# Sums of squares on VectorE for three means, and a pipelined embedding gate, in a two-layer decoder step

## Chip, cores and metric

The kernel runs on one core of one Trainium2 chip. The metric is the time on the device in microseconds (us), as the median of three executions. Beside those there is one profiled execution, from which all rows below come. TensorE is called PE, VectorE DVE, ScalarE ACT, GpSimd POOL and SyncE SP in the rows; PEld is TensorE's loading of weights.

## What is computed

The reference runs two layers of a decoder over 264 tokens (256 of a prompt, 8 single tokens) with a model width of 1024. In each layer a normalised input goes through one projection into three mixers, a shared output projection and a residual add; then comes a feed-forward block (dense in layer 0, eight experts in layer 1), and last an embedding gate. What the change touches is where the means of the squares for the norms are formed:

```python
def rmsnorm(x, g):
    xf = x.astype(jnp.float32)
    y = xf * lax.rsqrt(jnp.mean(xf * xf, axis=-1, keepdims=True) + EPS)
    return (y * g.astype(jnp.float32)).astype(x.dtype)
...
    h = h + y @ w_o
    h = h + ffn(rmsnorm(h, g_ffn))
    h = h + jax.nn.sigmoid(rmsnorm(h, g_ple) @ w_ple_gate) * (p_i @ w_ple_proj)
```

## The kernel before

The features lie on the 128 partitions, so that the state `h` is eight tiles ("chunks") of 128x264. The weights stream through a ring of three 2 MB slots in SBUF, in the order of their use. The mixers' projections of both layers and the output projection of layer 0 multiply the streamed weights as they are (`project_fp32`, L710). The others split each quarter of a slot first: ScalarE writes a rounded copy `whi` (L961), VectorE the remainder `wlo` (L1361, called by `low_upto`), three quarters ahead of TensorE, and `project` takes three products for each block (L734, L737, L738). The order of the work on each engine is the order in which the code of that engine is written; engines meet through semaphores.

A mean of squares goes over all 1024 features, that is over the partitions and over the eight chunks. ScalarE writes the square of each chunk into `sq`; `average` (L745) then multiplies the eight tiles of `sq` with a constant matrix of 1/1024 and sums them in one bank of PSUM. Each fp32 product shows as two passes in the trace, so a mean is 16 rows of L750. ScalarE takes the root (L944), VectorE its reciprocal (L1376), and the next block's results are scaled by it only when they are evacuated from PSUM (L1383, four banks in turn). So TensorE goes on with the next block's products right after `average` and needs for them only the gained rows of `h`, not the mean itself.

Three places matter, all at the end of a block of layer 0 or of the gate:

- **Boundary 1**, output projection to feed-forward block. For each chunk VectorE adds the result to `h` (`add_to_h`, L1388), writes the gained rows in two parts (`gain`, L1367 and L1368), and ScalarE squares the chunk (L1069).
- **Boundary 2**, feed-forward block to embedding gate: the same with ScalarE's L1094.
- **Boundary 3**, embedding gate of layer 0 to the mixers of layer 1. For each chunk VectorE evacuates the gate's product (`gate_out`, L1383), ScalarE takes the sigmoid (L1133), VectorE multiplies (L1701), adds to `h` (L1703) and writes the gained row for layer 1 (`mix_gain`, L1372); ScalarE squares (L1136, the last chunk L1142). In layer 0 VectorE evacuates chunk k and waits for its sigmoid before it does anything else. In layer 1 it evacuates chunk k+1 ahead of the rest of chunk k, and ScalarE loads the table of the root (L1140) before the last square instead of after it.

```python
for k in range(KD):                          # VectorE, embedding gate
    if l == 0 or k == 0:
        gate_out(k)
    if l and k + 1 < KD:
        low_upto(min(k + AHEAD + 1, KD), tail)
        gate_out(k + 1)
    dve.wait_ge(S["sig_ple"], k + 1)
    link(nc.vector.tensor_tensor(pp[:, k, :], pp[:, k, :], sig[:, k % 2, :], ALU.mult))
```

`link` makes VectorE wait for its own instruction before it issues the next.

Of the kernel before, what the change touches and what calls it, by code (L numbers as in the profile page):

```python
# [29 lines left out]
ALU = mybir.AluOpType  # L30
ACT = mybir.ActivationFunctionType
# [3 lines left out]
D_MODEL, SEQ, DEPTH, NB = 1024, 256, 2, 8  # L35
# [6 lines left out]
T = SEQ + NB  # L42
KD = D_MODEL // P
# [21 lines left out]
AHEAD = SPLITS - 1  # L65
# [80 lines left out]
def dense_quarters(chunk):  # L146

    return splits(min(NEED[chunk] + AHEAD, DENSE_Q))
# [7 lines left out]
def build(nc, wstream, x_in, p_in, par_in, state_in, y_out, a_prompt, a_sample, c_prompt, c_sample, v_sample):  # L156
    xn_rows = nc.dram_tensor("xn_rows", [T, ROW], F32, kind="Internal").ap()
    y_rows = nc.dram_tensor("y_rows", [1 + UNITS * CAP, D_MODEL], F32, kind="Internal").ap()
    with ExitStack() as ctx:
# [3 lines left out]
        def sem(name):  # L163
            return ctx.enter_context(nc.semaphore(name))
# [14 lines left out]
        sq = sb("sq", [P, KD, T])  # L179
# [17 lines left out]
        ones = {d: sb(f"ones_{d}", [P, P]) for d in (D_MODEL, D_A, D_B, 1)}  # L197
        before = sb("before", [P, P])
        ident = sb("ident", [P, P])
        eps = sb("eps", [P, 1])  # L200
# [53 lines left out]
        warm = cut(2)  # L254
# [8 lines left out]
        bank = [ctx.enter_context(nc.psum_tensor(f"bank{i}", [P, 512], F32)) for i in range(8)]  # L263
# [19 lines left out]
        tail = {n: sem(f"{n}_tail") for n in ("hi", "lo", "used")}  # L283
# [2 lines left out]
        dve_step = sem("dve_step")  # L286
        stored = sem("stored")
        flag_ready = sem("flag_ready")
        y_gained, y_pool, y_out_stored = (sem(n) for n in ("y_gained", "y_products_by_gpsimd", "y_out_stored"))


# [395 lines left out]
        def _(pe):  # L687
# [57 lines left out]
            def average(out, d, srcs, signal, waits=None):  # L745

                for k, s in enumerate(srcs):
                    if waits:
                        pe.wait_ge(waits[0], waits[1] + k)
                    mm = pe.matmul(out[:, 0:T], ones[d][:, :], s, start=(k == 0), stop=(k == len(srcs) - 1))  # L750
                mm.then_inc(signal, 1)

            def both(a, b, n):
                return [a[:, k, :] for k in range(n)], [b[:, k, :] for k in range(n)]

# [5 lines left out]
            pe.wait_ge(consts, 13)  # L761
            for l in range(DEPTH):
                S, B = L[l], BASE[l]
                average(bank[4], D_MODEL, [sq[:, k, :] for k in range(KD)], S["ms"], (S["sq_mix"], 1))
                project_fp32(B["zc"], N_ZC, gz, S["gh_mix"])
                project_fp32(B["zab"], 2 * CB, gz)

# [42 lines left out]
                else:  # L810
# [3 lines left out]
                        route_chunk(pe, k - 1)  # L814
                    route_chunk(pe, KD - 1)
                    route(pe)
                average(bank[4], D_MODEL, [sq[:, k, :] for k in range(KD)], S["ms"], (S["sq_ffn"], 1))
                if l == 0:

                    hids = both(hid_hi, hid_lo, KH)  # L820
# [25 lines left out]
                    at[0] = 0  # L846

                if l == 0:
                    average(bank[4], D_MODEL, [sq[:, k, :] for k in range(KD)], S["ms"], (S["sq_ple"], 1))
                    project(B["ple"], KD, *ghs, S["gh_ple"])  # L850
                else:
                    def square_mean(k):

                        pe.wait_ge(S["sq_ple"], k + 1)
                        mm = pe.matmul(bank[4][:, 0:T], ones[D_MODEL][:, :], sq[:, k, :], start=(k == 0), stop=(k == KD - 1))
                        if k == KD - 1:
                            mm.then_inc(S["ms"], 1)

                    assert LAST_BANKS[0] == B["ple"] % BANKS and LAST_BANKS[1] == 4
                    project(B["ple"], 1, *ghs, S["gh_ple"], tail, after=lambda k: k and square_mean(k - 1))  # L860
                    square_mean(KD - 1)
                    project(B["ple"] + 1, KD - 1, *ghs, S=tail)
# [78 lines left out]
        def _(act):  # L941
# [50 lines left out]
            for l in range(DEPTH):  # L992
# [134 lines left out]
                for k in range(KD):  # L1127
# [6 lines left out]
                    if k:  # L1134
                        act.wait_ge(made, k)
                        nc.scalar.activation(sq[:, k - 1, :], h[:, k - 1, :], ACT.Square).then_inc(done, 1)  # L1136
                        if l:
                            final_rows(k - 1)
                if l:
                    nc.scalar.activation(warm[:, 0:1], eps[:, :], ACT.Sqrt)  # L1140
                act.wait_ge(made, KD)
                nc.scalar.activation(sq[:, KD - 1, :], h[:, KD - 1, :], ACT.Square).then_inc(done, 1)  # L1142
            final_rows(KD - 1)
# [194 lines left out]
        def _(dve):  # L1338
# [16 lines left out]
            def low_upto(n, S=dense):  # L1355

                for i in range(done_lo[0], n):
                    q = SPLIT_Q[i] if S is dense else (PRE_MOE + N_EXP * UNIT_SLOTS) * QUARTERS + i
                    at = (i + SPLIT_AT if S is dense else i) % SPLITS
                    dve.wait_ge(S["hi"], i + 1)  # L1360
                    nc.vector.tensor_tensor(wlo[:, at, :], quarter_at(q), whi[:, at, :].bitcast(F32),  # L1361
                                            ALU.subtract).then_inc(S["lo"], 1)
                done_lo[0] = max(done_lo[0], n)

            def gain(l, name, k, signal, hi=gh_hi, lo=gh_lo):

                link(nc.vector.tensor_scalar(hi[:, k, :], h[:, k, :], col(l, name, k), None, ALU.mult))  # L1367
                nc.vector.scalar_tensor_tensor(lo[:, k, :], h[:, k, :], col(l, name, k), hi[:, k, :].bitcast(F32),  # L1368
                                               ALU.mult, ALU.subtract).then_inc(signal, 1)

            def mix_gain(l, k):
                nc.vector.tensor_scalar(gz[k], h[:, k, :], col(l, "g_mix", k), None, ALU.mult).then_inc(L[l]["gh_mix"], 1)  # L1372

# [23 lines left out]
            for l in range(DEPTH):  # L1397
# [189 lines left out]
                for k in range(KD):  # L1587
                    q = k - (KD - AHEAD)
                    if l and q >= 0:
                        dve.wait_ge(M["hi"], q + 1)  # L1590
                        nc.vector.tensor_tensor(wlo[:, q, :], quarter_at(q), whi[:, q, :].bitcast(F32),
                                                ALU.subtract).then_inc(M["lo"], 1)
                    add_to_h(B["wo"] + k, k)
                    if l == 0:
                        gain(l, "g_ffn", k, S["gh_ffn"])
                    else:
                        if k == KD - CB:
                            dve.wait_ge(S["tails"], 1)
                        nc.vector.tensor_scalar(g_rows[k], h[:, k, :], col(l, "g_ffn", k), None,
                                                ALU.mult).then_inc(F["normed"], 1)  # L1600
                    low_upto(dense_quarters(B["wo"] + k))
# [3 lines left out]
                if l == 0:  # L1605
# [6 lines left out]
                    for half, (ff, down) in enumerate((("ff", "down"), ("ff2", "down2"))):  # L1612
                        for f in range(KH):
                            n = half * KH + f


                            if n >= 2:
                                dve.wait_ge(S["silu"], n - 1)
                            evacuate(B[ff] + 2 * f, up[:, n % 2, :])
                            if f:  # L1620
                                hidden_low(n - 1)
                            low_upto(dense_quarters(B[ff] + 2 * f))
                            evacuate(B[ff] + 2 * f + 1, zb[:, n % 2, :])
                            dve.wait_ge(acc_evac, B[ff] + 2 * f + 2)
                            dve.wait_ge(S["silu"], n + 1)
                            nc.vector.tensor_tensor(zb[:, 2 + n % 2, :], zb[:, n % 2, :], sig[:, n % 2, :],
                                                    ALU.mult).then_inc(S["hid_f32"], 1)
                            if f < KH - 1:
                                low_upto(dense_quarters(B[ff] + 2 * f + 1))
                        hidden_low(half * KH + KH - 1)  # L1630
                        low_upto(dense_quarters(B[ff] + KF - 1))
                        for k in range(KD):
                            add_to_h(B[down] + k, k)
                            if half:
                                gain(l, "g_ple", k, S["gh_ple"])
                            low_upto(dense_quarters(B[down] + k))
                else:
                    route_tokens(dve, link, S)
# [50 lines left out]
                def gate_out(k):  # L1689
                    if k >= 2:  # L1690
                        dve.wait_ge(S["sig_ple"], k - 1)
                    evacuate(B["ple"] + k, up[:, k % 2, :])

                for k in range(KD):
                    if l == 0 or k == 0:
                        gate_out(k)
                    if l and k + 1 < KD:
                        low_upto(min(k + AHEAD + 1, KD), tail)
                        gate_out(k + 1)
                    dve.wait_ge(S["sig_ple"], k + 1)  # L1700
                    link(nc.vector.tensor_tensor(pp[:, k, :], pp[:, k, :], sig[:, k % 2, :], ALU.mult))  # L1701
                    if l + 1 < DEPTH:
                        link(nc.vector.tensor_tensor(h[:, k, :], h[:, k, :], pp[:, k, :], ALU.add))  # L1703
                        mix_gain(l + 1, k)
                        low_upto(dense_quarters(B["ple"] + k))
                    else:
                        nc.vector.tensor_tensor(h[:, k, :], h[:, k, :], pp[:, k, :], ALU.add).then_inc(S["y_fin_h"], 1)
# [110 lines left out]
```

## Time and profile before

| | before |
|---|---|
| median of 3 executions | 1105.1 us (1104.42 to 1105.19) |
| profiled execution, time on the device | 1104.26 us |
| its span, first to last instruction | 1102.6 us |
| TensorE busy | 1075.9 us, 98% of the span |
| VectorE, ScalarE busy | 891.0 us, 669.4 us |
| mean granted clock of TensorE | 0.993 of full |

The profiled execution lies 0.84 us under the median, and 1.66 us of its time lie outside the span. A row of a timeline gives the start in us from the span's start, the duration, the engine, the line of the kernel, the operation and its tiles, and in brackets how long the engine stood idle before it and what ended that. A row that ends in x16 merges 16 like instructions. The granted clock is given as a share of full speed: 1.00 is 2.4 GHz, 0.50 is 1.2 GHz.

### The profile page before, as it was taken

To read this page: it belongs to the slowest core of one execution; us is meant where nothing else is said; L and a number is where in the kernel's file an instruction comes from. 1 tells how busy PE (TensorE), PEld (TensorE's weight loads), DVE (VectorE), ACT (ScalarE), POOL (GpSimd) and SP (SyncE) were. 2 spreads that over 40 slices of the span, in tenths; PEclk is the share of its full clock that TensorE was granted. 3 is DMA by queue.
4 is the path that set the end of the run, shared out by engine and by line. 5 is a ranking of instruction groups with operands and counts; after the bars stand their busy time and mean duration, and the time that the engine had idled before them with its cause. 6 is when DMAs were issued, how large, how long until landed. Compare 5 with 4: busy or idle time off the path is not lost.

```text
span 1102.6 us, 16235 instructions
## 1 busy us (share of the span) xinstructions
PE 1075.9 (98%) x5901; PEld 930.0 (84%) x5901; DVE 891.0 (81%) x1257; ACT 669.4 (61%) x840; POOL 43.7 (4%) x58
## 2 busy tenths in 40 slices
PE   9998999999999998899999999999999999999996
PEld 8887899999999887788888888888888888888785
DVE  5897566566667889659989999899998999999785
ACT  2204344344454123548888788888888888887674
POOL 1000000000000000000000010000100001001100
PEclk9999999999999999899999999999999999999998
DMA  8432644645542442438999999999999999999910
GB/s 335 152 145 79 229 153 164 261 153 178 196 163 86 160 153 78 153 116 336 370 358 392 369 392 377 350 407 366 381 373 353 415 361 380 376 360 420 366 78 40
DMA packets 24197, 291.50 MB, mean 264 GB/s; under 512 B 3160, under 2 KB 3192, under 8 KB 7376
## 3 DMA queue, kind: packets, MB, share of 16 engines
q1 hardware_dynamic: 21040, 280.32, 66.5%
q0 software_dynamic: 3104, 10.46, 2.7%
q8 instruction: 34, 0.56, 0.2%
q14 instruction: 19, 0.16, 0.0%
HBM read 283.98 MB, written 6.79 MB: 264 GB/s over the span
## 4 chain that ended last, share of the span: by engine, by line
PE 88%; DMA 4%; DVE 3%; issue 2%; ACT 1%; POOL 1%; SPq 0%; POOLq 0%; DVEq 0%; ACTq 0%
PE bank L664 15%; PE bank L710 14%; PE bank L668 14%; PE bank L667 14%; PE bank L734 8%; PE bank L737 8%; PE bank L738 8%; PE bank L750 2%; DMA sq<-y_rows,row_id 2%; DMA y_rows<-work 1%; PE bank L608 1%; DVE rstd L1376 1%; DMA ring<-wstream 1%; PE bank L592 1%; PE bank L573 1%
## 5 line engine op out<-in xcount | busy, mean ns | idle before, releaser
L1271 DVE TENSOR_TENSOR wlo<-ring,whi 128x1024 fp32r<-128x1024 f32 x384 | 460.0, 1220 | 50.9 <-ACT whi L880 44.1
L880 ACT ACTIVATE whi<-ring 128x1024 fp32r<-128x1024 f32 x384 | 404.6, 1059 | 87.2 <-PE bank L664 71.4
L664 PE MATMUL bank<-whi,gh_hi 128*128 128x512 f32 x512 | 204.4, 399 | 0.1
L668 PE MATMUL bank<-whi,gh_lo 128*128 128x512 f32 x512 | 199.8, 390 | 0.0
L667 PE MATMUL bank<-wlo,gh_hi 128*128 128x512 f32 x512 | 199.5, 390 | 0.0
L734 PE MATMUL bank<-gh_hi,whi 128*128 128x264 f32 x480 | 138.0, 288 | 0.0
L737 PE MATMUL bank<-gh_lo,whi 128*128 128x264 f32 x480 | 136.0, 283 | 0.0
L738 PE MATMUL bank<-gh_hi,wlo 128*128 128x264 f32 x480 | 135.9, 283 | 0.0
L664 PEld LDWEIGHTS bank<-whi,gh_hi 128*128 128x128 f32 x512 | 96.2, 188 | 21.8 <-DVE wlo L1271 3.4
L668 PEld LDWEIGHTS bank<-whi,gh_lo 128*128 128x128 f32 x512 | 96.1, 188 | 20.9
L961 ACT ACTIVATE whi<-ring 128x1024 fp32r<-128x1024 f32 x87 | 91.1, 1050 | 35.0 <-PE bank L734 28.7
L667 PEld LDWEIGHTS bank<-wlo,gh_hi 128*128 128x128 f32 x512 | 96.3, 188 | 18.4
L710 PE MATMUL bank<-gz,ring 128*128 128x264 f32 x456 | 107.9, 386 | 0.1
L1361 DVE TENSOR_TENSOR wlo<-ring,whi 128x1024 fp32r<-128x1024 f32 x87 | 105.3, 1218 | 0.3
L664 PE MATMUL bank<-whi,hid_hi 128*128 128x512 f32 x256 | 102.9, 402 | 1.3 <-DVE wlo L1271 1.3
L668 PE MATMUL bank<-whi,hid_lo 128*128 128x512 f32 x256 | 101.0, 395 | 0.0
L667 PE MATMUL bank<-wlo,hid_hi 128*128 128x512 f32 x256 | 100.8, 394 | 0.0
L710 PEld LDWEIGHTS bank<-gz,ring 128*128 128x128 f32 x456 | 86.5, 190 | 15.5 <-DMA ring<-wstream 0.8
L734 PEld LDWEIGHTS bank<-gh_hi,whi 128*128 128x128 f32 x480 | 90.4, 188 | 0.6 <-issue 0.3
L737 PEld LDWEIGHTS bank<-gh_lo,whi 128*128 128x128 f32 x480 | 90.5, 188 | 0.3
L738 PEld LDWEIGHTS bank<-gh_hi,wlo 128*128 128x128 f32 x480 | 90.0, 187 | 0.0
L1432 DVE SCALAR_TENSOR_TENSOR cv<-cpad,par,cv 128x256 f32<-128x256 f32 x180 | 76.9, 479 | 1.4
(253 smaller groups left out, 1371.6 us busy)
## 6 DMA issues: line engine op xcount, KB each, us to landing
ring<-wstream SPq DMA_DIRECT2D x130, 2048.0 KB, 8.5
y_rows<-work POOLq DMA_DIRECT2D x7, 512.0 KB, 8.0
ring<-wstream SPq DMA_DIRECT2D x1, 1536.0 KB, 10.4
h<-x_in SPq DMA_DIRECT2D x2, 528.0 KB, 4.1
y_out<-work SPq DMA_DIRECT2D x2, 528.0 KB, 3.0
xn_rows<-work SPq DMA_DIRECT2D x2, 512.5 KB
par<-par_in SPq DMA_DIRECT2D x2, 494.5 KB, 7.6
c_sample<-xc POOLq DMA_DIRECT2D x2, 372.0 KB, 3.9
```

The lines of the kernel that those rows point to most:

```text
L664: mm = pe.matmul(out[:, :], xh, whi[:, pos, cols_], start=(k == 0), stop=False)
L667: pe.matmul(out[:, :], xh, wlo[:, pos, cols_], start=False, stop=False)
L668: mm = pe.matmul(out[:, :], xl, whi[:, pos, cols_], start=False, stop=(k == last))
L710: mm = pe.matmul(bank[c % BANKS][:, 0:T], quarter_at(q)[:, w * P:(w + 1) * P], rows[k], start=(k == 0), stop=(k == len(rows) - 1))
L734: mm = pe.matmul(out, wh, hi[k], start=(k == 0), stop=False)
L737: pe.matmul(out, wh, lo[k], start=False, stop=False)
L738: mm = pe.matmul(out, wl, hi[k], start=False, stop=(k == len(hi) - 1))
L880: nc.scalar.activation(whi[:, q % SPLITS, :], quarter_at(q), ACT.Copy).then_inc(S["hi"], 1)
L961: nc.scalar.activation(whi[:, at, :], quarter_at(q), ACT.Copy).then_inc(S["hi"], 1)
L1271: v.tensor_tensor(wlo[:, q % SPLITS, :], quarter_at(q), whi[:, q % SPLITS, :].bitcast(F32), ALU.subtract).then_inc(S["lo"], 1)
L1361: nc.vector.tensor_tensor(wlo[:, at, :], quarter_at(q), whi[:, at, :].bitcast(F32), ALU.subtract).then_inc(S["lo"], 1)
L1432: last[c] = tick(nc.vector.scalar_tensor_tensor(dst, src, wc[:, c, k:k + 1], dst, ALU.mult, ALU.add))
```

## The change

VectorE gets a new step, `sum_square`, that adds a chunk's square into the first tile of `sq`, in place. At boundaries 1 and 2 it adds chunks 1 to 6, one per chunk, right behind `gain` of the following chunk; at boundary 3 it adds chunks 1 to 5, two chunks late. TensorE's new `average_of_sum` waits for the last of these sums and multiplies the sum and the chunks that are left, so two tiles at boundaries 1 and 2, three at boundary 3, in place of eight. The gate of layer 0 takes the order of layer 1: `gate_out(k + 1)` is issued ahead of the rest of chunk k. ScalarE loads the table of the root before the last square in layer 0 also. The means at the start of layer 0, in the feed-forward block of layer 1 and at the end stay as they were.

```diff
@@ TensorE
+            def average_of_sum(signal, ready, n=KD - 1):
+
+                sums[0] += n - 1
+                pe.wait_ge(sq_sum, sums[0])
+                pe.matmul(bank[4][:, 0:T], ones[D_MODEL][:, :], sq[:, 0, :], start=True, stop=False)
+                for k in range(n, KD):
+                    pe.wait_ge(ready, k + 1)
+                    mm = pe.matmul(bank[4][:, 0:T], ones[D_MODEL][:, :], sq[:, k, :], start=False, stop=(k == KD - 1))
+                mm.then_inc(signal, 1)
...
-                average(bank[4], D_MODEL, [sq[:, k, :] for k in range(KD)], S["ms"], (S["sq_mix"], 1))
+                if l == 0:
+                    average(bank[4], D_MODEL, [sq[:, k, :] for k in range(KD)], S["ms"], (S["sq_mix"], 1))
+                else:
+                    average_of_sum(S["ms"], S["sq_mix"], KD - 2)
...
-                average(bank[4], D_MODEL, [sq[:, k, :] for k in range(KD)], S["ms"], (S["sq_ffn"], 1))
+                if l == 0:
+                    average_of_sum(S["ms"], S["sq_ffn"])
+                else:
+                    average(bank[4], D_MODEL, [sq[:, k, :] for k in range(KD)], S["ms"], (S["sq_ffn"], 1))
...
-                    average(bank[4], D_MODEL, [sq[:, k, :] for k in range(KD)], S["ms"], (S["sq_ple"], 1))
+                    average_of_sum(S["ms"], S["sq_ple"])
@@ ScalarE
-                if l:
-                    nc.scalar.activation(warm[:, 0:1], eps[:, :], ACT.Sqrt)
+                nc.scalar.activation(warm[:, 0:1], eps[:, :], ACT.Sqrt)
                 act.wait_ge(made, KD)
                 nc.scalar.activation(sq[:, KD - 1, :], h[:, KD - 1, :], ACT.Square).then_inc(done, 1)
@@ VectorE
+            def sum_square(ready, k):
+
+                if 1 <= k < KD - 1:
+                    dve.wait_ge(ready, k + 1)
+                    if k > 1:
+                        dve.wait_ge(sq_sum, sums[0])
+                    sums[0] += 1
+                    nc.vector.tensor_tensor(sq[:, 0, :], sq[:, 0, :], sq[:, k, :], ALU.add).then_inc(sq_sum, 1)
...
                         gain(l, "g_ffn", k, S["gh_ffn"])
+                        sum_square(S["sq_ffn"], k - 1)
...
                                 gain(l, "g_ple", k, S["gh_ple"])
+                                sum_square(S["sq_ple"], k - 1)
...
                 for k in range(KD):
-                    if l == 0 or k == 0:
+                    if k == 0:
                         gate_out(k)
-                    if l and k + 1 < KD:
-                        low_upto(min(k + AHEAD + 1, KD), tail)
+                    if k + 1 < KD:
+                        if l:
+                            low_upto(min(k + AHEAD + 1, KD), tail)
                         gate_out(k + 1)
+                    if l == 0:
+                        low_upto(dense_quarters(B["ple"] + k))
+                        sum_square(L[1]["sq_mix"], k - 2)
                     dve.wait_ge(S["sig_ple"], k + 1)
```

On TensorE at boundary 1, before (the output projection, the mean, the first products of the feed-forward block):

```order
L710 MATMUL bank<-work,ring 128x264 x64
L750 MATMUL bank<-sq,ones 128x264 x8
L734 MATMUL bank<-gh_hi,whi 128x264
L737 MATMUL bank<-gh_lo,whi 128x264
L738 MATMUL bank<-gh_hi,wlo 128x264
```

and of the change:

```order
L711 MATMUL bank<-work,ring 128x264 x64
L760 MATMUL bank<-sq,ones 128x264
L763 MATMUL bank<-sq,ones 128x264
L735 MATMUL bank<-gh_hi,whi 128x264
L738 MATMUL bank<-gh_lo,whi 128x264
L739 MATMUL bank<-gh_hi,wlo 128x264
```

Six of the eight products of the mean are gone; the first that is left reads the sum.

On VectorE at boundary 3, the last two chunks of the gate of layer 0 (`up` is the evacuated product, `small` holds the gained rows of the last two chunks), before:

```order
L1383 TENSOR_TENSOR up<-bank,rstd 128x264
L1701 TENSOR_TENSOR pp<-pp,sig 128x264
L1703 TENSOR_TENSOR h<-h,pp 128x264
L1372 TENSOR_SCALAR small<-h,par 128x264
L1383 TENSOR_TENSOR up<-bank,rstd 128x264
L1701 TENSOR_TENSOR pp<-pp,sig 128x264
L1703 TENSOR_TENSOR h<-h,pp 128x264
L1372 TENSOR_SCALAR small<-h,par 128x264
```

and of the change:

```order
L1412 TENSOR_TENSOR up<-bank,rstd 128x264
L1398 TENSOR_TENSOR sq<-sq 128x264
L1736 TENSOR_TENSOR pp<-pp,sig 128x264
L1738 TENSOR_TENSOR h<-h,pp 128x264
L1401 TENSOR_SCALAR small<-h,par 128x264
L1398 TENSOR_TENSOR sq<-sq 128x264
L1736 TENSOR_TENSOR pp<-pp,sig 128x264
L1738 TENSOR_TENSOR h<-h,pp 128x264
L1401 TENSOR_SCALAR small<-h,par 128x264
```

The evacuation at the top of the second piece is that of the last chunk: the work of the last but one chunk now stands behind it, and two sums stand between.

## Rows read from the trace of the kernel before

**Rows 1.** Chain that ended last, in order of time (start, us, what): boundaries 1, 2.

```profile
127.30 3.56 PE bank L750 x16
322.68 3.56 PE bank L750 x16
```

**Rows 2.** Timeline of all engines, boundary 1.

```profile
127.13 3.72 PE L750 MATMUL bank<-sq,ones 128*128 128x264 f32 x16
...
128.19 0.49 DVE L1368 SCALAR_TENSOR_TENSOR gh_lo<-h,par,gh_hi 128x264 fp32r<-128x264 f32 x1
128.60 1.22 DVE L1361 TENSOR_TENSOR wlo<-ring,whi 128x1024 fp32r<-128x1024 f32 x1
130.50 0.48 PE L734 MATMUL bank<-gh_hi,whi 128*128 128x264 f32 x1
```

**Rows 3.** Timeline of DVE, boundary 2 and the gate of layer 0.

```profile
323.58 0.49 DVE L1368 SCALAR_TENSOR_TENSOR gh_lo<-h,par,gh_hi 128x264 fp32r<-128x264 f32 x1
...
343.68 0.43 DVE L1703 TENSOR_TENSOR h<-h,pp 128x264 f32<-128x264 f32 x1
344.15 0.36 DVE L1372 TENSOR_SCALAR gz<-h,par 128x264 f32<-128x264 f32 x1
344.42 1.22 DVE L1361 TENSOR_TENSOR wlo<-ring,whi 128x1024 fp32r<-128x1024 f32 x1
...
351.66 0.36 DVE L1372 TENSOR_SCALAR small<-h,par 128x264 f32<-128x264 f32 x1
```

**Rows 4.** Timeline of PE, from boundary 2 to the mixers of layer 1.

```profile
325.88 0.48 PE L734 MATMUL bank<-gh_hi,whi 128*128 128x264 f32 x1
...
349.16 0.28 PE L738 MATMUL bank<-gh_hi,wlo 128*128 128x264 f32 x1
349.28 3.96 PE L750 MATMUL bank<-sq,ones 128*128 128x264 f32 x16
353.08 2.83 PE L710 MATMUL bank<-gz,ring 128*128 128x264 f32 x12
```

**Rows 5.** Timeline of ACT, boundary 3.

```profile
352.05 0.42 ACT L1142 ACTIVATE sq<-h 128x264 f32<-128x264 f32 x1 [1.04 <-DVE small L1372]
352.49 1.28 ACT L944 ACT_TABLE_LOAD   x1
```

**Rows 6.** Timelines of PE, DVE and ACT, end of the gate of layer 1.

```profile
1088.20 0.28 PE L738 MATMUL bank<-gh_hi,wlo 128*128 128x264 f32 x1
...
1088.59 0.43 DVE L1383 TENSOR_TENSOR up<-bank,rstd 128x264 f32<-128x264 f32 x1 [1.66 <-PE bank L738]
1088.94 0.42 DVE L1701 TENSOR_TENSOR pp<-pp,sig 128x264 f32<-128x264 f32 x1
1089.39 0.43 DVE L1707 TENSOR_TENSOR h<-h,pp 128x264 f32<-128x264 f32 x1
...
1090.71 1.28 ACT L1140 ACT_TABLE_LOAD   x1
1092.00 0.20 ACT L1140 ACTIVATE small<-eps 128x1 f32<-128x1 f32 x1
1092.11 0.41 ACT L1142 ACTIVATE sq<-h 128x264 f32<-128x264 f32 x1
```

**Rows 7.** Timeline of PE, mixers of layer 1.

```profile
429.20 1.16 PE L710 MATMUL bank<-pe_in,ring 128*128 128x264 f32 x4 [2.10 <-DVE work L1383]
...
441.68 1.60 PE L750 MATMUL bank<-sq,ones 128*128 128x264 f32 x6 [0.82 <-ACT sq L1036]
445.98 0.59 PE L734 MATMUL bank<-hid_hi,whi 128*128 128x264 f32 x1 [2.70 <-ACT pp L972]
```

**Rows 8.** Windows: stretch, us, busy of five engines, PEclk, DMA share, GB/s.

```profile
430.00:435.00 5.00, 3.68 (x25) 3.10 (x24) 3.97 (x11) 2.87 (x6) 1.29 (x2) 1.00 0.05 8
...
445.00:446.00 1.00, 0.02 (x1) 0.03 (x1) 0.95 (x1) 0.92 (x4) 0.00 (x0) 0.78 0.99 426
...
452.00:453.00 1.00, 1.00 (x9) 1.00 (x8) 0.60 (x2) 0.17 (x1) 0.00 (x0) 0.80 0.02 4
```

More of the change, by code:

```diff
@@ L288, in build @@
         flag_ready = sem("flag_ready")
+        sq_sum = sem("squares_summed")
         y_gained, y_pool, y_out_stored = (sem(n) for n in ("y_gained", "y_products_by_gpsimd", "y_out_stored"))
@@ L751, in average @@
                 mm.then_inc(signal, 1)
+            sums = [0]
+            def average_of_sum(signal, ready, n=KD - 1):
[6 more added lines that the diff above has]
+                mm.then_inc(signal, 1)
             def both(a, b, n):
@@ L1369, in gain @@
                                                ALU.mult, ALU.subtract).then_inc(signal, 1)
+            sums = [0]
+            def sum_square(ready, k):
[5 more added lines that the diff above has]
+                    nc.vector.tensor_tensor(sq[:, 0, :], sq[:, 0, :], sq[:, k, :], ALU.add).then_inc(sq_sum, 1)
             def mix_gain(l, k):
```

## The prediction

> **What bounds the kernel now.** I read the chain that ended last first: both means at the ends of layer 0's blocks stand on it, with 3.56 us of TensorE each [rows 1]. So a pass of L750 costs 3.56 / 16 = 0.2225 us, a product of two passes 0.445 us. Then I read the timelines around the three boundaries, because a product taken off the chain only helps if TensorE has something else to do at that moment. At boundary 1 TensorE starts the mean at 127.13, while VectorE is still working on the last chunk: its `gh_lo` starts at 128.19, and the next block's first product runs at 130.50 [rows 2]. So the first products of the mean are done in time in which the last chunk is not ready anyway. At boundary 3 this is plainer: the gate's last product starts at 349.16 and ends at 349.44, the last gained row of VectorE starts at 351.66, its square ends at 352.05 + 0.42 = 352.47, and the mixers' first product starts at 353.08 [rows 3 to 5]. The mean and the mixers there wait for the last square, not for the number of products. From the release by that square to the next block's first product it takes 353.08 - 352.47 = 0.61 us with one product of the mean in between. The roots and reciprocals behind a mean are not on the path, since TensorE goes on into four free banks.
>
> **The change part by part.**
>
> *Boundaries 1 and 2.* TensorE now can't start before the sum of chunks 0 to 6, and that is VectorE's last instruction there. `gh_lo` takes 128.60 - 128.19 = 0.41 us until the next instruction starts [rows 2], so the sum starts at 128.60. The trace has no such sum; the nearest row is the add of two SBUF tiles of the same size into `h`, 0.43 us [rows 3], and I take that; its start-to-start step, 0.35 us as with the evacuation to the product in layer 1 [rows 6], is the lower bound where something follows. The sum ends at 129.03. With two products behind it, 0.61 + 0.445 = 1.06 us, the next block starts at 130.09 instead of 130.50: **-0.41 us**. At boundary 2 the sum starts at 323.58 + 0.41 = 323.99, ends at 324.42, and the gate starts at 325.48 instead of 325.88 [rows 3, 4]: **-0.40 us**. The five earlier sums of each boundary lie in time in which VectorE waits for TensorE; without that cover each would cost its 0.35 to 0.43 us. The remainder `wlo` that follows the sum starts 0.43 us later, and is made three quarters ahead: nothing.
>
> *Boundary 3, the order of the gate.* The end of layer 1's gate shows this order without sums. I count from the end of the gate's last product. The last evacuation starts at 1088.59 - (1088.20 + 0.28) = 0.11 [rows 6]. Behind it on VectorE stand, in order: a sum (at 0.11 + 0.35 = 0.46), the product of chunk 6 (0.81), the add (0.81 + 0.45 = 1.26, the step 1089.39 - 1088.94 of [rows 6]), the gained row (1.26 + 0.47 = 1.73, the step 344.15 - 343.68 of [rows 3]), the last sum (0.27 later, 344.42 - 344.15, so 2.00 to 2.43), the product of chunk 7 (2.35), the add (2.80), the gained row (3.27 to 3.63). Before, chunk 6 was already finished when chunk 7 was evacuated. ScalarE can square chunk 6 when its gained row ends, at 1.73 + 0.36 = 2.09: 2.13 to 2.55. Then comes the table, 1.28 us [rows 5, 6], from 2.57 to 3.85, the one-element root 0.01 behind it, and the last square 0.11 after that (1092.11 - 1092.00): 3.97 to 4.39. The mixers start 0.61 later, at 5.00, where before they start at 353.08 - 349.44 = 3.64: **+1.36 us**. Of this 0.31 is the table, which now stands ahead of the last square; without it the square would end at 3.63 + 0.03 + 0.42 = 4.08. The rest is the two sums and the product, add and gained row of chunk 6 that now stand behind the last evacuation. The 1.28 us saved behind the mean buy nothing, since the root is off the path.
>
> Within the gate, VectorE's work for a chunk is 0.35 + 1.22 + 0.35 + 0.45 + 0.47 + 0.27 = 3.11 us against TensorE's 24 products of 0.12 (349.28 - 349.16 [rows 4]) = 2.9 us. It falls behind by 0.2 per chunk over the two chunks that have both a sum and a split. The split for chunk k+3 now starts when chunk k+1 is done and takes 0.35 + 1.22 = 1.6 of the 2.9 us that chunk k+2 runs: covered; if that were wrong, TensorE would stall by up to 0.5.
>
> Here a rule of the skill speaks against the early table. The instruction behind the load of layer 1 starts 0.01 us after its end [rows 6]. The Trainium skill (ScalarE: Activation LUTs, "What ACT_TABLE_LOAD costs") adds a drain of about 1.38 us to every load; by that the last square would come 1.38 us later still and the sum would be 1.9 instead of 0.55. The row decides.
>
> So the plain sum is -0.41 - 0.40 + 1.36 = **+0.55 us**.
>
> *What the idle time does to TensorE's clock.* This is the larger term. At boundary 3 TensorE now has nothing to multiply from 0 to the last sum's end at 2.43, plus about 0.2 for loading weights: 2.6 to 2.7 us, then a short burst, then it waits again. The trace has three waits to hold beside that. After 2.10 us of idle at 429.20, and after 0.82 at 441.68, the granted clock stayed at 1.00; around 2.70 us of idle, from 443.28 (441.68 + 1.60) to 445.98, it fell to 0.50 [rows 7, 8]. The windows date it: 0.78 in the stretch from 445 gives a fall at 445.56, 0.80 in the one from 452 a rise at 452.40. That is 6.84 us at half speed, beginning 2.28 us into the wait. Boundary 3's wait is nearest to the one of 2.70, so I take the clock to fall there in the same way: half speed from 2.28 to 9.12. On the path in it lies what follows the last square, from about 4.6 to 9.12; 4.5 us at half speed lose 2.25. Bounds: 0 if the clock holds, 6.84 / 2 = 3.4 if all of it falls into unbroken work. At boundaries 1 and 2 TensorE idles from 127.30 [rows 1] to about 129.25, 1.95 us, nearest to the 2.10 that left the clock alone: 0, with an upper end of 3.4 each, rather 1.5, since the work behind is unbroken while at 448 TensorE was held up again.
>
> **Sum:** 0.55 + 2.25 = +2.8 us, 1104.26 to 1107.1 for the profiled execution. That execution lies 0.84 under the median, so against the median: 1105.1 + 2.8 = **1107.9 us**.
>
> **The rivals.**
>
> *A, the clock holds* (not slower): the mechanism is the wait at boundary 3 and whether TensorE's burst of two products in the middle of it is enough. It decides at one point, whether the clock in the window behind the gate stays at 1.00. For it: 2.10 us did no harm, and the 2.70 of the trace was preceded by other idle time; against it: boundary 3's two waits add up to more than the 2.70. It gives 0.55: 1105.65, within what can be measured. The Trainium skill (TensorE: Matmul & The Clock Gate, "Why this matters for your kernels") warns of longer gaps than any of these; by that rule A would be the outcome, and the fall at 445 in this trace speaks against it.
>
> *B, the clock falls at boundary 1 or 2 also*: 1.95 us is close to the longest harmless wait and not far from the harmful one. Each costs about 1.5: 1109.4 with one, 1110.9 with both.
>
> *C, the products come off in full*: 6 + 6 + 5 = 17 products of 0.445 are 7.6 us, 1097.5. All of them stand on the chain; but it would need the sums ready when TensorE arrives, and the last one is issued behind the last chunk's gained rows. What the change says of itself holds on TensorE, but its wait takes the place of the products.
>
> *D, the drain of the early table without a fall of the clock*: 1.9, so 1107.0.
>
> **How the numbers follow.** My forecast 0.46, A 0.26, B 0.22, C 0.03, D 0.03. What a measurement of this kernel can tell from no change is about 0.2%, 2.2 us. The forecast's own range, 1.9 to 3.9 for a loss of 1.4 to 3.4 by the clock, lies over 2.2 in four cases of five: 0.37. With B 0.22 and a little of D, slower has 0.60. Faster has C and a hundredth of A: 0.04. The rest, 0.36, is no difference. The range must hold A, the forecast and B: from 1105.65 less 0.6 for the uncertain steps of VectorE, 1105.0, to 1110.9.
>
> **What would show it.** Right: rows of the mean fall from 16 to 4, 4 and 6 at the three boundaries; TensorE's next block starts 1.0 to 1.1 us after the last sum at boundaries 1 and 2; the mixers of layer 1 start about 5 us after the gate's last product instead of 3.64, with the table's load just ahead of the last square; and the granted clock reads 0.50 for some us behind boundary 3. Wrong: a clock of 1.00 there (A), one of 0.50 behind 129 or 325 (B), an idle TensorE inside the gate for want of `wlo`, or a first product of a block that follows the one before by less than the 2.8 us that boundaries 1 and 2 should take.

## The result, and the profile after

The changed kernel takes 1107.86 us (median of 13 executions, 1104.42 to 1109.76); the kernel before, run beside it, takes 1104.49 (13 executions, 1103.03 to 1106.53). The ratio is 1.0021, with a 95% interval of 1.0013 to 1.003: slower by 2.3 us (the ratio compares the two kernels round by round; the two medians lie 3.4 us apart). The forecast was 1107.9, with a range of 1105.0 to 1110.9 and 0.60 on slower.

The profiled execution of the changed kernel is one of the shortest, 1104.54 us against 1104.26 before, and its clock holds at all three boundaries. So its rows show the plain steps. First the page: busy time, share and instructions of each engine.

```profile
PE 1068.9 (97%) x5867; PEld 923.7 (84%) x5867; DVE 897.0 (81%) x1274; ACT 670.3 (61%) x841; POOL 44.8 (4%) x58
```

TensorE is busy for 7.0 us less than before (1075.9), and the span, 1102.9 us, has not become shorter (1102.6): the products went, and idle time came. The timeline of TensorE at boundaries 1, 2 and 3 shows it (start, us, engine, line, operation, and in brackets the idle time before and what ended it):

```profile
128.78 0.71 PE L760 MATMUL bank<-sq,ones 128*128 128x264 f32 x2 [1.78 <-DVE sq L1398]
129.33 0.61 PE L763 MATMUL bank<-sq,ones 128*128 128x264 f32 x2
129.58 0.48 PE L735 MATMUL bank<-gh_hi,whi 128*128 128x264 f32 x1
...
323.55 0.71 PE L760 MATMUL bank<-sq,ones 128*128 128x264 f32 x2 [1.79 <-DVE sq L1398]
...
324.35 0.48 PE L735 MATMUL bank<-gh_hi,whi 128*128 128x264 f32 x1
...
347.64 0.28 PE L739 MATMUL bank<-gh_hi,wlo 128*128 128x264 f32 x1
350.40 0.71 PE L760 MATMUL bank<-sq,ones 128*128 128x264 f32 x2 [2.48 <-DVE sq L1398]
...
352.34 0.71 PE L763 MATMUL bank<-sq,ones 128*128 128x264 f32 x2 [0.78 <-ACT sq L1160]
352.89 2.83 PE L711 MATMUL bank<-gz,ring 128*128 128x264 f32 x12
...
356.45 2.83 PE L711 MATMUL bank<-gz,ring 128*128 128x264 f32 x12
```

The 16 rows of a mean are now 4, 4 and 6, and TensorE waits 1.78, 1.79 and 2.48 us for a sum of VectorE, and 0.78 more for the last square. At boundary 3 the mixers start 352.89 - (347.64 + 0.28) = 4.97 us behind the gate's last product, where it was 3.64 before [rows 4]. At boundary 1 VectorE's timeline has the sum right behind the last chunk's second gained row:

```profile
127.89 0.49 DVE L1386 SCALAR_TENSOR_TENSOR gh_lo<-h,par,gh_hi 128x264 fp32r<-128x264 f32 x1
128.30 0.42 DVE L1398 TENSOR_TENSOR sq<-sq 128x264 f32<-128x264 f32 x1
```

Why the last square at boundary 3 is later stands in the timelines there, first of VectorE, then of ScalarE:

```profile
348.03 0.43 DVE L1412 TENSOR_TENSOR up<-bank,rstd 128x264 f32<-128x264 f32 x1 [0.68 <-PE bank L739]
...
351.19 0.36 DVE L1401 TENSOR_SCALAR small<-h,par 128x264 f32<-128x264 f32 x1
```

```profile
350.48 1.28 ACT L1158 ACT_TABLE_LOAD   x1
351.77 0.20 ACT L1158 ACTIVATE small<-eps 128x1 f32<-128x1 f32 x1
```

Between the last evacuation and the last gained row there now stand two sums and the whole rest of chunk 6. The table's load ends at 351.76, after the last gained row (351.55), so it too is on the path, by 0.2 to 0.3 us. In this execution the clock holds. A window of boundary 3 (stretch, us, busy of five engines, PEclk, DMA share, GB/s):

```profile
352.00:354.00 2.00, 1.66 (x7) 1.44 (x8) 0.41 (x2) 1.18 (x3) 0.00 (x0) 1.00 0.03 8
```

There is one more wait, at a place that the change does not touch: behind the experts of layer 1, at the first product of its gate. Here is that product, first before, where nothing stands idle ahead of it, then of the change; and under them, in the same order, the branch of TensorE's sequencer (PEldq) that leads past work not needed here (`pe.If(some > 0)`; the line gives its duration three times, in ns, and its start):

```profile
1061.45 0.36 PE L734 MATMUL bank<-gh_hi,whi 128*128 128x264 f32 x1
...
1061.74 0.36 PE L735 MATMUL bank<-gh_hi,whi 128*128 128x264 f32 x1 [1.36 <-DVE gh_lo L1684]
```

```profile
L837 PEldq COMPARE_BRANCH  x1: 3502/3502/3502, 1057.8 to 1057.8; - x1
...
L856 PEldq COMPARE_BRANCH  x1: 4792/4792/4792, 1056.8 to 1056.8; - x1
```

Before, the branch lasts 3.50 us and ends under the experts' last products. In the change it lasts 4.79 us and ends at about 1061.6, and the gate starts 0.2 us later; the first `gh_lo`, all that this product needs of VectorE, had ended at 1059.55. So TensorE loses 1.36 us. Why the branch lasts longer is not shown.

### The profile page after: what moved, and what is told of

Its sections match the earlier page's. It is cut to its first block, busy times and chain, and to the rows that moved or that the text cites. A ratio compares the mean times of both kernels' runs of the same rounds, so it can differ in the third digit from the quotient of the medians.

```text
span 1102.9 us, 16199 instructions
## 1 busy us (share of the span) xinstructions
PE 1068.9 (97%) x5867; PEld 923.7 (84%) x5867; DVE 897.0 (81%) x1274; ACT 670.3 (61%) x841; POOL 44.8 (4%) x58
## 4 chain that ended last, share of the span: by engine, by line
PE 91%; DVE 4%; ACT 2%; DMA 1%; issue 1%; POOL 0%; DVEq 0%; ACTq 0%; POOLq 0%
PE bank L665 16%; PE bank L669 15%; PE bank L668 15%; PE bank L711 14%; PE bank L735 8%; PE bank L738 8%; PE bank L739 8%; PE bank L751 2%; DMA ring<-wstream 1%; PE bank L609 1%; DVE rstd L1405 1%; DVE wlo L1289 1%; PE bank L593 1%; PE bank L574 1%; PE bank L532 0%
## 5 line engine op out<-in xcount | busy, mean ns | idle before, releaser
L739 PE MATMUL bank<-gh_hi,wlo 128*128 128x264 f32 x480 | 136.0, 283 | 0.0
L739 PEld LDWEIGHTS bank<-gh_hi,wlo 128*128 128x128 f32 x480 | 90.0, 187 | 0.0
```

The costliest lines, as they stand in the source:

```text
L739: mm = pe.matmul(out, wl, hi[k], start=False, stop=(k == len(hi) - 1))
```

## The experiments

The theory was the forecast's: the plain steps come out near nothing, and what makes the median slower is the clock, which falls behind boundary 3 in part of the executions. Rivals: A, the clock holds and the plain steps are dearer than worked out; B, it falls at boundaries 1 and 2 also; D, the early table costs a drain. Line numbers of TensorE and VectorE shift by a few lines from kernel to kernel. The first four ran in one session (before: 1105.38, 30 executions), the others in a second (before: 1104.63, 29 executions).

### The change once more

> The changed kernel as it is, once more. One profiled execution of it read 1104.54 us with a granted clock of 1.00 behind all three boundaries, while the median of its thirteen executions was 1107.86 and their spread 5.3 us. Theory (the clock falls in most executions, not in all): the median is again 1107 to 1109 with a spread of 4 us or more; if the profiled execution is one of the long ones, its windows show 0.50 for some us behind boundary 3 or boundary 1 or 2, and its span exceeds 1102.9 us by what those stretches cost. Rival (the added time is in the work itself, at some place that the profile of the short execution hides): a long execution shows the clock at 1.00 behind the boundaries and longer waits elsewhere.

Measured: 1107.09 us (1104.82 to 1109.91, 12 executions), ratio 1.0020 [1.0008, 1.0031]. This profiled execution has what that of the first did not. Windows and TensorE's timeline at boundary 3:

```profile
350.00:351.00 1.00, 0.48 (x1) 0.45 (x2) 0.97 (x4) 0.82 (x2) 0.00 (x0) 0.81 0.00 0
351.00:352.00 1.00, 1.00 (x4) 0.67 (x2) 0.96 (x4) 0.99 (x2) 0.00 (x0) 0.50 0.00 0
```

```profile
347.76 0.28 PE L739 MATMUL bank<-gh_hi,wlo 128*128 128x264 f32 x1
350.52 1.19 PE L760 MATMUL bank<-sq,ones 128*128 128x264 f32 x2 [2.48 <-DVE sq L1398]
...
357.33 2.83 PE L711 MATMUL bank<-gz,ring 128*128 128x264 f32 x12
```

The clock falls at 350.62 (0.81 in the stretch from 350 means 0.38 us at half speed), within the wait, and is back at 354.02 (0.99 in the stretch from 354): 3.40 us at half speed. From the gate's last product to the second group of the mixers it takes 357.33 - 347.76 = 9.57 us, where the other execution of the same program takes 356.45 - 347.64 = 8.81: this fall costs 0.76. Most of it lies beside the wait for the last square. The wait behind the experts is in this execution too, 1.39 us.

### Filling the waits

```diff
+            def fill(n):
+                for _ in range(n):
+                    pe.matmul(bank[7][:, 0:P], ones[1][:, :], ones[1][:, :], start=True, stop=True)
+
             def average_of_sum(signal, ready, n=KD - 1):
 
                 sums[0] += n - 1
+                fill(7 if n == KD - 1 else 10)
                 pe.wait_ge(sq_sum, sums[0])
...
                 for k in range(n, KD):
+                    if n < KD - 1 and k == KD - 1:
+                        fill(3)
                     pe.wait_ge(ready, k + 1)
```

> The changed kernel with idle TensorE work in the waits: 7 products of two constant 128x128 tiles ahead of the wait for the sum at boundaries 1 and 2 (about 1.5 us each), 10 ahead of it at boundary 3 and 3 ahead of the last square there. Their results are not used. Theory (clock): the plain sum is left, +0.55 us against before, so a ratio of 1.0003 to 1.0010, a spread as small as before's (about 3 us) and a clock of 1.00 behind all three boundaries. Rival (work): the time stays where the change left it, 1.002 or more, as the filler takes nothing away that VectorE or ScalarE do.

Measured: 1105.64 us (1102.76 to 1106.54, 12 executions), 1.0002 [0.9991, 1.0013]. The granted clock is 1.00 behind all three boundaries. TensorE's timeline at boundary 3:

```profile
348.20 0.28 PE L739 MATMUL bank<-gh_hi,wlo 128*128 128x264 f32 x1
348.32 2.39 PE L758 MATMUL bank<-ones 128*128 128x128 f32 x20
350.96 0.71 PE L765 MATMUL bank<-sq,ones 128*128 128x264 f32 x2 [0.25 <-DVE sq L1405]
...
357.01 1.28 PE L711 MATMUL bank<-gz,ring 128*128 128x264 f32 x5
```

The path there is the same, 357.01 - 348.20 = 8.81 us; only the idle time is filled, with products that nobody reads. The slowdown of 1.0020 of the change beside it goes to 1.0002: 2.0 us less, though the two intervals still touch between 1.0008 and 1.0013. But the filling did not take away the falls alone. Behind the experts the profiled execution has

```profile
1063.20 0.36 PE L735 MATMUL bank<-gh_hi,whi 128*128 128x264 f32 x1 [0.42 <-issue]
```

where the change waits 1.36 and 1.39: about 1 us of the 2.0 comes from there, and the rest is within this run's noise. So this run by itself does not show that the clock is what makes the median slower. At the boundaries rival A falls, since the windows at 0.50 of the runs on either side of this one show the clock fall there; behind the experts the plain steps are dearer than worked out, as A has it.

### The sums of boundaries 1 and 2 alone

The two `average_of_sum` of `sq_ffn` and `sq_ple` and their sums stay; boundary 3 is as before (eight products, the old order of the gate, the late table).

> Only boundaries 1 and 2 of the change: the sums and the products of two tiles there; the gate's order, the mean at boundary 3 and the table as before. Plain sum -0.81 us. Theory with the clock falling at boundary 3 alone: 0.9990 to 0.9995. Rival B (it falls at boundaries 1 or 2 also, after 1.8 us of idle): each fall costs about 1.5 us, so 1.000 to 1.002, a spread wider than before's, and a stretch of 0.50 behind 129 or 325 in the profile of a long execution.

Measured: 1104.87 us (1101.9 to 1106.62, 12 executions), 1.0000 [0.9989, 1.0011]; the profiled execution has 1.00 behind both boundaries. The interval takes in both the theory's gain and rival B's loss of it: this run alone settles nothing between them.

### Boundary 3 alone

```diff
-                if l == 0:
-                    average_of_sum(S["ms"], S["sq_ffn"])
-                else:
-                    average(bank[4], D_MODEL, [sq[:, k, :] for k in range(KD)], S["ms"], (S["sq_ffn"], 1))
+                average(bank[4], D_MODEL, [sq[:, k, :] for k in range(KD)], S["ms"], (S["sq_ffn"], 1))
...
-                        sum_square(S["sq_ffn"], k - 1)
...
-                                sum_square(S["sq_ple"], k - 1)
```

(and `average` for `sq_ple` likewise.)

> Only boundary 3 of the change: the gate's order, its five sums, the mean of three tiles and the early table; boundaries 1 and 2 as before. Plain sum +1.36 us. Theory with the clock falling at boundary 3: 1.36 + 2.25, so 1.0025 to 1.0040. If most of the added time comes from boundaries 1 and 2 by the clock (rival B): 1.0010 to 1.0020.

Measured: 1108.4 us (1107.47 to 1109.49, 7 executions), 1.0033 [1.002, 1.0045]. Windows and TensorE's timeline:

```profile
353.00:354.00 1.00, 0.33 (x1) 0.33 (x2) 0.42 (x1) 0.61 (x3) 0.00 (x0) 0.82 0.00 0
354.00:355.00 1.00, 1.00 (x3) 0.79 (x3) 0.00 (x0) 0.04 (x1) 0.00 (x0) 0.50 0.00 0
...
357.00:358.00 1.00, 1.00 (x6) 0.87 (x5) 0.34 (x1) 0.00 (x0) 0.00 (x0) 0.98 0.00 0
```

```profile
348.97 0.28 PE L739 MATMUL bank<-gh_hi,wlo 128*128 128x264 f32 x1
...
353.67 1.25 PE L763 MATMUL bank<-sq,ones 128*128 128x264 f32 x2 [0.79 <-ACT sq L1157]
...
359.43 1.94 PE L711 MATMUL bank<-gz,ring 128*128 128x264 f32 x8
```

Here the fall comes with the second wait: half speed from 353.64 to 357.04, again 3.40 us. It lies almost wholly in unbroken work, and costs 359.43 - 348.97 - 8.81 = 1.65 us, nearly half its length. So a fall of the same length costs 0.76 or 1.65, by where it lies. This is the run that shows the clock's part most plainly, as its trace has no wait behind the experts: the mean granted clock of its seven executions is 0.9911, that of the kernel before beside it 0.9929, which is about 4.0 us more at half speed. If all of it lay in unbroken work it would lose 2.0 us (standard error 0.8), and with the 1.33 of the plain steps that makes 3.3 of the 3.6 us measured. The kernel lacks what boundaries 1 and 2 save (below).

### The order of the gate alone

Boundaries 1 and 2 as before; at boundary 3 the pipelined order of the gate stays, without sums, with eight products and the late table.

> Only the order of the gate of layer 0 is the change's (evacuation of chunk k+1 ahead of the rest of chunk k); no sums, eight products in every mean, the table late as before. By the steps of the prediction without the two sums and without the table: the mixers' first product 4.0 us behind the gate's last product's end instead of 3.64, so +0.35 us. TensorE has seven products for that wait, so by the clock theory nothing is lost there: a ratio of 0.9995 to 1.0010 and a clock of 1.00 from 348 to 358. Rival (the new order of the gate is what lengthens it, by VectorE or ScalarE): 1.0020 or more.

Measured: 1105.5 us (1103.5 to 1108.2, 12 executions), 1.0007 [0.9997, 1.0016]. TensorE at boundary 3:

```profile
349.54 0.28 PE L739 MATMUL bank<-gh_hi,wlo 128*128 128x264 f32 x1
...
353.27 0.71 PE L751 MATMUL bank<-sq,ones 128*128 128x264 f32 x2 [0.34 <-ACT sq L1155]
```

The mixers start at 353.82, 4.00 us behind the gate's end: of the 1.33 at this boundary the order alone is 0.36, the sums and the table the rest. The wait is 0.34 here, with products up to it.

### The change with the late table

```diff
-                nc.scalar.activation(warm[:, 0:1], eps[:, :], ACT.Sqrt)
+                if l:
+                    nc.scalar.activation(warm[:, 0:1], eps[:, :], ACT.Sqrt)
```

> The change without the early table in layer 0: the root's table is loaded behind the last square, as before. By the prediction's steps the last square ends 0.31 us earlier (4.08 instead of 4.39 behind the gate's last product's end), the mixers start at 4.7 instead of 5.0, and the clock falls as often: a ratio of 1.0005 to 1.0025, 0.3 us under the change, which the profile shows sooner than the times. By the skill's drain of 1.38 us it would be 1.7 us under the change.

Measured: 1106.15 us (1104.78 to 1108.92, 12 executions), 1.0015 [1.0006, 1.0023]. ScalarE at boundary 3:

```profile
354.23 1.28 ACT L963 ACT_TABLE_LOAD   x1
355.53 0.48 ACT L963 ACTIVATE root<-bank,eps 128x264 f32<-128x264 f32 x1
```

The last square, ahead of these, ends 4.09 us behind the gate's end (350.12), and the mixers start at 354.82, 4.70 behind it instead of 4.97: the early table costs 0.27 us. Rival D falls. The next activation starts 0.02 us after a load's end here, and 0.01 after it in the change's own rows (351.76 to 351.77). The drain of 1.38 us that the Trainium skill (ScalarE: Activation LUTs, "What ACT_TABLE_LOAD costs") adds is seen in neither.

This profiled execution shows rival B's event, a fall at boundary 2. Windows and TensorE's timeline:

```profile
324.00:325.00 1.00, 0.87 (x3) 0.67 (x4) 1.00 (x2) 0.57 (x1) 0.00 (x0) 0.69 1.03 442
...
327.00:328.00 1.00, 1.00 (x7) 1.00 (x7) 1.00 (x1) 0.98 (x2) 0.00 (x0) 0.60 0.00 0
```

```profile
324.13 1.05 PE L760 MATMUL bank<-sq,ones 128*128 128x264 f32 x2 [1.79 <-DVE sq L1399]
...
328.07 0.29 PE L739 MATMUL bank<-gh_hi,wlo 128*128 128x264 f32 x1
```

Half speed from 324.38 to 327.80, 3.42 us. The fourth L739 of the gate starts at 328.07, 3.94 us behind the mean's first product; in the profile of the change it starts at 325.88, 2.33 behind it. The fall costs 1.61. At boundary 3 this execution has the waits of 2.48 us and, for the last square, 0.50, and its clock stays at 1.00. Behind the experts it waits 1.38.

### The means moved into the wait

If TensorE waits for a sum that nobody needs at once, the next block's first chunk can go ahead of it. The change, with each of its three means behind the first chunk of the following block:

```diff
-                if l == 0:
-                    average_of_sum(S["ms"], S["sq_ffn"])
-                else:
+                if l:
                     average(bank[4], D_MODEL, [sq[:, k, :] for k in range(KD)], S["ms"], (S["sq_ffn"], 1))
...
-                    project(B["ff"], KF, *ghs, S["gh_ffn"])
+                    project(B["ff"], 1, *ghs, S["gh_ffn"])
+                    average_of_sum(S["ms"], S["sq_ffn"])
+                    project(B["ff"] + 1, KF - 1, *ghs)
```

(likewise `project(B["ple"], ...)` and, in layer 1, `project_fp32(B["zc"], ...)`.)

> The change with each of its three means moved behind the first chunk of the next block's products, so that TensorE has work while VectorE and ScalarE finish; the scaling by the mean happens only at the evacuation. Theory (the products come off only where TensorE does not wait for the sum): boundaries 1 and 2 cost TensorE the two products alone, 0.89 us instead of 3.4, so -2.5 each; at boundary 3 its first chunk starts at once and waits about 0.5 for the last gained row, then 1.3 for three products, so -1.55: 6.6 us in all, a ratio of 0.993 to 0.995, and a clock of 1.00 behind the boundaries. Rival (the later root and reciprocal hold up the evacuation, so that TensorE waits for a bank): 0.997 or more.

Measured: 1098.83 us (1097.92 to 1100.9, 5 executions), 0.9953 [0.994, 0.9966]: 5.2 us faster than the kernel before, and the quickest kernel of this study; a little short of what was expected, with which the interval agrees. TensorE at boundary 3:

```profile
343.80 0.28 PE L739 MATMUL bank<-gh_hi,wlo 128*128 128x264 f32 x1
...
347.77 0.71 PE L711 MATMUL bank<-small,ring 128*128 128x264 f32 x2 [0.57 <-DVE small L1403]
...
349.65 1.72 PE L711 MATMUL bank<-gz,ring 128*128 128x264 f32 x7
```

At boundary 1 the timeline has no idle time left, at boundary 3 0.57 us, for the last gained row itself. The mixers' second chunk starts 349.65 - 344.08 = 5.57 us behind the gate's end; in the change's own profile it starts 356.45 - 347.92 = 8.53 behind it. The first line here is the same product in the trace of the kernel before, the second the gate's first product in layer 1, in this kernel:

```profile
356.64 2.83 PE L710 MATMUL bank<-gz,ring 128*128 128x264 f32 x12
...
1055.10 0.36 PE L735 MATMUL bank<-gh_hi,whi 128*128 128x264 f32 x1 [1.45 <-DVE gh_lo L1686]
```

Behind the three boundaries the kernel is 356.64 - 349.65 = 6.99 us ahead, a little more than the 6.6 expected; what it is short of in the end, 1.45, is the wait behind the experts.

### The place alone, with eight products

The kernel before, its three means moved to the same places, all eight products kept and the gate in its old order.

> The kernel before with the three means moved behind the first chunk of the next block, and nothing of the change: eight products each, no sums, the old order of the gate. Theory: the sixteen passes of a mean, 3.56 us, are then all on TensorE's path, where before 3.37 to 3.64 were: 0.9995 to 1.0005. It tells whether a gain of the previous kernel comes from the place of the mean alone (then this one has it too) or from sums and place together.

Measured: 1107.33 us (1105.62 to 1108.79, 11 executions), 1.0026 [1.0017, 1.0035]: slower, and the expectation missed. VectorE in the gate of layer 0:

```profile
330.38 1.80 DVE L1384 RECIPROCAL rstd<-root 128x264 f32<-128x264 f32 x1 [4.50 <-ACT root L952]
332.22 0.43 DVE L1391 TENSOR_TENSOR up<-bank,rstd 128x264 f32<-128x264 f32 x1
...
335.49 0.42 DVE L1391 TENSOR_TENSOR up<-bank,rstd 128x264 f32<-128x264 f32 x1
...
337.61 1.22 DVE L1369 TENSOR_TENSOR wlo<-ring,whi 128x1024 fp32r<-128x1024 f32 x1
...
354.63 0.36 DVE L1380 TENSOR_SCALAR small<-h,par 128x264 f32<-128x264 f32 x1
```

The later mean makes the reciprocal late, so VectorE begins the gate's evacuations late (332.22), and the old order takes 335.49 - 332.22 = 3.27 us for a chunk, of which 0.49 is the wait for the chunk's own sigmoid. TensorE needs 2.9, but each chunk now waits for its remainder `wlo`, which VectorE makes in the same loop (this one ends at 337.61 + 1.22 = 338.83):

```profile
338.97 0.36 PE L734 MATMUL bank<-gh_hi,whi 128*128 128x264 f32 x1
342.23 0.36 PE L734 MATMUL bank<-gh_hi,whi 128*128 128x264 f32 x1
```

So VectorE's 3.26 us become TensorE's pace (342.23 - 338.97), and the last gained row ends at 354.99, 3.10 us behind the gate's last product (351.61 + 0.28); the mixers' first chunk waits for it, and then comes a mean of 3.72 us. In the version before this one the pipelined order makes up the delay. Its gain comes from three things together: short means, their place, and the order of the gate. How it divides among them was not tried further.

## Why the prediction was right

**The plain steps.** At the three boundaries the mechanism is as forecast. The +1.36 at boundary 3 measured +1.33, of which the table 0.27 (0.31 was said) and the order without sums 0.36. Nothing of the five earlier sums, of the remainder or of the gate's inside showed on TensorE's path. The two other boundaries came out better than worked out. From the start of the last `gh_lo` to the next block's first product it was 130.50 - 128.19 = 2.31 us before at boundary 1 [rows 2]; now it is 129.58 - 127.89 = 1.69, so -0.62 where -0.41 was said. At boundary 2 it was 325.88 - 323.58 = 2.30 [rows 3, 4] and is 324.35 - 322.66 = 1.69 (the last is the start of `gh_lo` in the same timeline), so -0.61 where -0.40 was said. The step that was off is the 1.06 us from the last sum to the next block: it measures 129.58 - (128.30 + 0.42) = 0.86, because the first product of the block follows the mean's second tile by 0.25 (129.33 to 129.58), where behind the last square at boundary 3, from which the 0.61 came, it is 0.55 (352.34 to 352.89 now). The plain sum of the boundaries is thus -0.62 - 0.61 + 1.33 = +0.10 instead of +0.55. What the forecast did not have is the wait behind the experts, about +1.4. It stands in the four profiled executions of kernels with all the sums and no filling (the two of the change 1.36 and 1.39, late table 1.38, moved means 1.45), is 0.42 in the filled one, and is in none of the others; the forecast left out what lies behind the mixers of layer 1, without a word on it.

**The clock.** That TensorE's new idle time can bring its clock down was the forecast's largest term, and the falls are shown: windows at 0.50 behind a boundary in three of the five profiled executions of kernels with open waits (the change twice, sums alone, boundary 3 alone, late table). The term was **mis-sized**. "4.5 us at half speed lose 2.25" was taken from a stretch of 6.84 us [rows 8], and for every execution. The stretches here last 3.40, 3.40 and 3.42 us, cost 0.76, 1.65 and 1.61, and come in a part of the executions, at boundary 2 also (rival B, whose 1.5 for one fall was close to the 1.61). What they come to can be estimated from the mean granted clock of every execution. In the first session it averages 0.9929 for the kernel before, 0.9922 for the change and 0.9938 for the filled kernel. Twice the part that is missing to 1, times the span, is the time at half speed: 15.6, 17.3 and 13.8 us. A part of each lies at the kernel's very end, where TensorE has little to multiply, and is taken to be the same on average. If all of the difference lay in unbroken work, half of it would be lost: 0.9 us (standard error 0.3) of the change against before, 1.8 (0.5) against the filled kernel.

**The sum.** So the 2.3 us are +0.10 at the boundaries, about +1.4 behind the experts and, by this estimate, up to 0.9 by the clock, where the forecast had +0.55 and +2.25. That the total came out at the forecast's value is luck: a clock term more than twice too large stood in for a wait that the sum did not have. No experiment takes that wait away by itself, so its part rests on the traces.

**The median and its spread.** The change spreads over 5.3 us (1104.42 to 1109.76), the kernel before beside it over 3.5; in the next session it was 5.1 against 4.7, so the spread tells little. That the profiled execution of the change stands only 0.28 us from that of before, with the wait behind the experts in it, has another reason: it was 0.3 us ahead before boundary 1, and it gained 0.95 in the experts of layer 1, where all nine other profiles are quicker than that of before, by 0.4 to 1.2. How often the clock falls at each boundary stays open: the run with boundaries 1 and 2 alone has too wide an interval, and a profile shows one execution only.

**Rival C**, all 7.6 us: TensorE's busy time did fall by 7.0, and its wait took their place, as the rival's own words had it. The saving is to be had where the mean does not stand in TensorE's way: 5.2 us in the kernel with the means moved.

## What to carry to other kernels

Products taken off an engine that then waits for the same data buy only what is not waited for (here 0.6 of 2.7 us at a boundary), and idle time on TensorE can cost its clock on top. Before the number of products is cut, look for the instruction that stands first in TensorE's queue without being needed there: moved behind work that is ready, it covers the wait. A move of that kind delays whoever waits for it (here root, reciprocal, evacuation, and with them the remainders that TensorE needs), so see that this engine has the slack to catch up. And compare the whole trace, not only the places that were changed: by the traces, more than half of the loss here came up 700 us behind the last of them.

## What was not expected of the hardware

A branch on TensorE whose code was not changed took 3.39 to 3.68 us in five kernels, 3.97 in the filled one and 4.79 to 4.87 in three others; on what that hangs is open.

The same wait did not have the same effect twice. A wait of 1.79 us at boundary 2 left the clock at 1.00 in the change's profile and was followed by a fall in the run with the late table; one of 2.48 at boundary 3 was followed by a fall 2.58 us after the idle time began in one execution (350.62 - 348.04), 4.39 after it in another kernel (353.64 - 349.25), and by none in a third. Nor is the 2.10 us wait in the mixers of layer 1 harmless, which the forecast took it for [rows 7, 8]. In three other kernels it is followed by a fall; this is the one with the sums of boundaries 1 and 2 alone:

```profile
427.89 1.16 PE L711 MATMUL bank<-pe_in,ring 128*128 128x264 f32 x4 [2.08 <-DVE work L1410]
...
430.00:431.00 1.00, 1.00 (x7) 1.00 (x6) 0.03 (x1) 0.51 (x1) 0.67 (x2) 0.50 0.00 0
```

So the forecast's way of pricing, by the nearest wait that did or did not bring a fall, gives what can happen and not what will. The Trainium skill (TensorE: Matmul & The Clock Gate, "Why this matters for your kernels") warns only of gaps longer than any of these; the rows at 0.50 here speak against that as a safe limit.
